# A projection stage with a five-tap convolution: its loop written out, its last tile handled in four column pieces

## What is computed

```python
h = rms_norm(x, norm_w[l])
proj = h @ w_in[l].astype(h.dtype)
...
qkv = jax.nn.silu(centred_depthwise_conv(jnp.concatenate([q, k, v], axis=-1), conv_w))
...
def centred_depthwise_conv(x, w):
    pad = (w.shape[0] - 1) // 2
    return lax.conv_general_dilated(
        x, w[:, None, :].astype(x.dtype), window_strides=(1,), padding=[(pad, pad)],
        dimension_numbers=('NWC', 'WIO', 'NWC'), feature_group_count=x.shape[-1])
```

## Time and profile before

| | us |
|---|---|
| median of three runs | 3618.07 |
| profiled execution | 3623.07 |
| its traced span | 3621.2 |
| TensorE busy in the span | 3216.5 |
| first and last matmul of `project_conv` start | 58.90, 340.10 |
| last store of `project_conv` issued | 355.23 |
| first load of `rows_prepare` issued | 360.85 |

### The profile page before, as it was taken

How to read it: one execution, slowest core, us unless ns; L and a number is a source line. 1 busy time by engine, 2 the same in 40 slices (tenths; PEclk the granted TensorE clock), 3 DMA queues, 4 the chain that set the end, 5 groups by cost and what they waited for, 6 DMA issues and landing times. The chain is left out here.

```text
span 3621.2 us, 60742 instructions
## 1 busy us (share of the span) xinstructions
PE 3216.5 (89%) x24054; PEld 2670.9 (74%) x24054; DVE 1305.8 (36%) x2502; ACT 1110.3 (31%) x2246; POOL 346.9 (10%) x344
## 2 busy tenths in 40 slices
PE   6997998886999989889599988999899969959799
PEld 5776897666999976468487777888688846648687
DVE  5454442253555536655500001221000035543333
ACT  4222332243444438711411110000111147730132
POOL 0000000232333320033000000000000011120000
PEclk8998999996999989989799999999999979979899
DMA  3221763342334333155411111110111141054443
GB/s 111 70 70 58 247 229 138 99 135 88 126 128 133 127 105 113 55 170 194 142 58 65 63 62 47 35 35 23 70 70 70 67 158 50 14 183 163 186 150 122
DMA packets 237171, 382.65 MB, mean 106 GB/s; under 512 B 37440, under 2 KB 158016, under 8 KB 227520
## 3 DMA queue, kind: packets, MB, share of 16 engines
q1 hardware_dynamic: 194848, 343.95, 27.7%
q10 hardware_dynamic: 42144, 36.18, 3.1%
HBM read 237.98 MB, written 142.08 MB: 105 GB/s over the span
## 5 line engine op out<-in xcount | busy, mean ns | idle before, releaser
L106 PE MATMUL ps_pp<-h_hi,ps_whi 128*128 128x512 f32 x512 | 200.2, 391 | 15.1 <-DVE ps_wlo L2360 15.1
L106 PE MATMUL gc_pp<-h_hi,gc_whi 128*128 128x512 f32 x512 | 200.3, 391 | 13.1 <-DVE gc_wlo L2453 13.1
L107 PE MATMUL gc_pp<-h_lo,gc_whi 128*128 128x512 f32 x512 | 200.1, 391 | 0.0
L107 PE MATMUL ps_pp<-h_lo,ps_whi 128*128 128x512 f32 x512 | 199.9, 390 | 0.0
L108 PE MATMUL ps_pp<-h_hi,ps_wlo 128*128 128x512 f32 x512 | 199.9, 390 | 0.0
L108 PE MATMUL gc_pp<-h_hi,gc_wlo 128*128 128x512 f32 x512 | 199.9, 390 | 0.0
L106 PE MATMUL pc_pp<-h_hi,pc_whi 128*128 128x512 f32 x384 | 153.5, 400 | 19.7 <-DVE pc_wlo L327 19.7
L107 PE MATMUL pc_pp<-h_lo,pc_whi 128*128 128x512 f32 x384 | 152.7, 398 | 0.0
L108 PE MATMUL pc_pp<-h_hi,pc_wlo 128*128 128x512 f32 x384 | 152.5, 397 | 0.0
L1865 POOL COPY ca_q<-ca_qr 128x512 f32 (+1 forms) x16 | 10.1, 630 | 1406.7 <-DMA ca_vr<-scratch_v_rows 1231.4
L1999 DVE CUSTOM_DVE_ANT_0 ca_neg<-ca_s,ca_bias 128x640 f32<-128x640 f32 (+4 forms) x128 | 92.0, 738 | 104.7 <-PE ca_s L1886 102.9
(11 more groups left out here) (337 smaller groups left out, 7917.1 us busy)
## 6 DMA issues: line engine op xcount, KB each, us to landing
ds_pk<-scratch_pack SPq DMA_DIRECT2D x32, 1280.0 KB, 7.7
scratch_pack<-rp_out SPq DMA_DIRECT2D x32, 512.0 KB, 2.7
scratch_sig_fm<-ps_ob SPq DMA_DIRECT2D x16, 1024.0 KB, 3.9
mb_sg<-scratch_sig_fm SPq DMA_DIRECT2D x16, 1024.0 KB, 6.9
scratch_qkv_fm<-pc_acc SPq DMA_DIRECT2D x12, 1024.0 KB, 4.8
rp_fm<-scratch_qkv_fm SPq DMA_DIRECT2D x96, 128.0 KB, 2.8
n_x<-in_x SPq DMA_DIRECT2D x16, 512.0 KB, 4.0
scratch_pack<-rp_out SPq DMA_DIRECT2D x32, 256.0 KB, 2.5
```

Source lines behind the costliest of these rows:

```text
L106: nc.tensor.matmul(out, ah, bh, start=(first and i == 0), stop=False)
L107: nc.tensor.matmul(out, ah, bl, start=False, stop=False)
```

## The change

The stage's programs are written out in Python, tile by tile, without a loop of the chip. Four things differ in what they do:

1. Weights are loaded as soon as `raw[s]` is free: up to three tiles ahead, and ahead of the store in SyncE's program.
2. ScalarE and VectorE split tile n + 2 in front of their work on tile n. ScalarE does so right after the product of tile n is done, VectorE ahead of the convolution of tile n.
3. The taps of all 12 tiles come in one load of 128 by 12 by 5 (60 floats to a partition, gathered from 12 places of 20 bytes), behind the first two weight loads. `w_in` counts the weights alone.
4. The last tile is signalled by TensorE, copied, convolved, put through SiLU and stored in four column pieces. The copies take 512 columns each; the convolved pieces are 510, 512, 512 and 514 columns wide, since a piece needs two columns of its right neighbour.

```diff
-        taps = [c.sb(f"taps{s}", [P, DN_TAPS]) for s in range(2)]
+        taps = c.sb("taps", [P, DN_TILES, DN_TAPS])
...
+        cols = [slice(g * NCOL, (g + 1) * NCOL) for g in range(GROUPS)]
+        ends = [NCOL * (g + 1) - PAD for g in range(GROUPS - 1)] + [SEQ]
+        pieces = [slice(a, b) for a, b in zip([0] + ends[:-1], ends)]
...
+            def load(n):
+                s = n % 2
+                if n >= 2:
+                    sp.wait_ge(lo_ready[s], n // 2 + START)
+                sp.dma_start(raw[s][:], w_tiles[n]).then_inc(w_in[s], 16)
+
+            load(0)
+            load(1)
+            sp.dma_start(taps[:], conv_w.rearrange("n p t -> p n t")).then_inc(taps_in, 16)
+            load(2)
+            for n in range(LAST):
+                s = n % 2
+                if n + 3 <= LAST:
+                    load(n + 3)
+                sp.wait_ge(silu_done[s], n // 2 + 1 + START)
+                sp.dma_start(out[n], acc[s][:]).then_inc(stored[s], 16)
+            for g, at in enumerate(pieces):
+                sp.wait_ge(piece_silu[g], 1 + START)
+                sp.dma_start(out[LAST][:, at], acc[LAST % 2][:, at]).then_inc(stored[LAST % 2], 16)
...
+            for n in range(LAST):
+                s = n % 2
+                act.wait_ge(product[s], n // 2 + 1 + START)
+                if n + 2 <= LAST:
+                    split_hi(n + 2)
+                nc.scalar.copy(pre[s][:, PAD:PAD + SEQ], pp[s][:]).then_inc(copied[s], 1)
+                act.wait_ge(tap_done[s], (n // 2 + 1) * DN_TAPS + START)
+                nc.scalar.activation(acc[s][:], acc[s][:], ACT.Silu).then_inc(silu_done[s], 1)
+            s = LAST % 2
+            for g in range(GROUPS + 1):
+                if g < GROUPS:
+                    act.wait_ge(piece_product[g], 1 + START)
+                    nc.scalar.copy(pre[s][:, PAD + g * NCOL:PAD + (g + 1) * NCOL],
+                                   pp[s][:, cols[g]]).then_inc(piece_copied[g], 1)
+                if g > 0:
+                    act.wait_ge(piece_tap[g - 1], DN_TAPS + START)
+                    at = pieces[g - 1]
+                    nc.scalar.activation(acc[s][:, at], acc[s][:, at], ACT.Silu).then_inc(piece_silu[g - 1], 1)
...
+            for n in range(LAST):
+                s = n % 2
+                if n + 2 <= LAST:
+                    split_lo(n + 2)
+                dve.wait_ge(copied[s], n // 2 + 1 + START)
+                dve.wait_ge(stored[s], 16 * (n // 2) + START)
+                convolve(n, slice(0, SEQ), tap_done[s], (n // 2) * DN_TAPS)
+            s = LAST % 2
+            dve.wait_ge(stored[s], 16 * (LAST // 2) + START)
+            for g, at in enumerate(pieces):
+                dve.wait_ge(piece_copied[g], 1 + START)
+                convolve(LAST, at, piece_tap[g], 0)
...
+            for g, at in enumerate(cols):
+                split_products(nc, pp[s][:, at], [(whi[s][:, k, :], wlo[s][:, k, :], hi[:, k, at], lo[:, k, at])
+                                                  for k in range(KT)]).then_inc(piece_product[g], 1)
```

More of the change, by code:

```diff
@@ L277, in project_conv @@
         stored = c.sems("stored", 2)
+        piece_product = c.sems("piece_product", GROUPS)
+        piece_copied = c.sems("piece_copied", GROUPS)
+        piece_tap = c.sems("piece_tap", GROUPS)
+        piece_silu = c.sems("piece_silu", GROUPS)
         block = c.stack.enter_context(nc.Block())
-        N = DN_TILES // 2
+        cols = [slice(g * NCOL, (g + 1) * NCOL) for g in range(GROUPS)]
+        ends = [NCOL * (g + 1) - PAD for g in range(GROUPS - 1)] + [SEQ]
+        pieces = [slice(a, b) for a, b in zip([0] + ends[:-1], ends)]
@@ L302, in _, with split_hi @@
+            sp.wait_ge(stored[0], 16 * (DN_TILES // 2) + START)
+            sp.wait_ge(stored[1], 16 * (DN_TILES // 2 - 1 + GROUPS) + START)
         @block.scalar
         def _(act):
-            def split_hi(j, s):
-                act.wait_ge(w_in[s], 32 * j + 32 + START)
+            def split_hi(n):
+                s = n % 2
+                act.wait_ge(w_in[s], 16 * (n // 2) + 16 + START)
                 nc.scalar.copy(whi[s][:], raw[s][:]).then_inc(hi_ready[s], 1)
[L308 to L321, removed]
+            for n in range(2):
+                split_hi(n)
+            for n in range(LAST):
[6 more added lines that the diff above has]
+                nc.scalar.activation(acc[s][:], acc[s][:], ACT.Silu).then_inc(silu_done[s], 1)
@@ L323, in _, with split_lo @@
         @block.vector
         def _(dve):
-            def split_lo(j, s):
-                dve.wait_ge(hi_ready[s], j + 1 + START)
+            def split_lo(n):
+                s = n % 2
+                dve.wait_ge(hi_ready[s], n // 2 + 1 + START)
                 nc.vector.tensor_tensor(wlo[s][:], raw[s][:], whi[s][:].bitcast(F32),
                                         ALU.subtract).then_inc(lo_ready[s], 1)
[L330 to L340, removed]
-                    if more:
-                        split_lo(j + 1, s)
@@ new lines, in convolve @@
+            def convolve(n, at, sem, base):
+                s = n % 2
+                nc.vector.tensor_scalar(acc[s][:, at], pre[s][:, at], taps[:, n, 0:1], None, ALU.mult).then_inc(sem, 1)
+                for t in range(1, DN_TAPS):
+                    dve.wait_ge(sem, base + t + START)
+                    nc.vector.scalar_tensor_tensor(out=acc[s][:, at], in0=pre[s][:, at.start + t:at.stop + t],
+                                                   scalar=taps[:, n, t:t + 1], in1=acc[s][:, at], op0=ALU.mult,
+                                                   op1=ALU.add).then_inc(sem, 1)
```

24 lines of the change are left out of this document (14 added, 10 removed).

## The result

The changed kernel takes 3606.11 us, the median of 20 runs (3595.32 to 3620.73), against 3622.99 us for the kernel before, also of 20 runs (3612.68 to 3640.07). The ratio is 0.9949, with a 95% interval from 0.9937 to 0.9961. It is faster, by 17 us instead of the 26 forecast, and its time lies 2 us above the range. The profiled execution of the changed kernel took 3617.24 us, 11 us more than the median, with a span of 3615.5 us; so single stages are read from it, and the whole from many executions. Three executions of kernels cut behind the scan (further down) are marked slow on record, being over 1.5% above the fastest of their set, and are kept in the means; without them the changed kernel up to the scan has a mean of 1386.0 us instead of 1387.9, and its shifted version 1390.2 instead of 1392.8.

What follows compares the result with a forecast made beforehand. TensorE, busy for 89% of the span, was taken as the bound, losing time to stalls, low clock and the stage's end. Gains of 18.2, 7.8 and 0.3 us took the 3618.07 us median to 3591.8, range 3584 to 3604.

Steps and rivals of the forecast that it cites:

- Part 1: Stalls between the changed stage's tiles: early loads and splits remove them, gain 18.2 us: 10.2 idle time, 8.0 clock.
- the rival in which its clock stays low: Parts 1 and 2 come, but TensorE still falls to 1.2 GHz now and then in the stage: 3600; chance 0.08.
- the sum: Whole kernel: 18.2 + 7.8 + 0.3 = 26.3 us gained, later stages starting earlier and otherwise the same.
- Part 2: Changed stage's end: the last tile in four pieces ends the stage earlier, gain 7.8 us.
- Part 3: Taps in one load: the first CAST no longer waits for them, gain 0.3 us; the new load costs nothing.
- Part 4: Written-out code in the changed stage: TensorE steps through 1152 matmuls without a loop, code loading put at nothing.
- The rival with slow code: TensorE's code arrives too slowly without a loop; at 50 ns more a matmul the kernel takes 3650; chance 0.04.

Runs made afterwards that it cites:

- shifted version: Changed kernel cut behind the scan, with 133 semaphore increments on TensorE spread over four gaps to move its code: mean 1392.8 us.
- tail only: Kernel before with items 3 and 4 alone, written out, weights asked for and split where the kernel before does: 3614.24 us, ratio 0.9967.
- the cut kernels: Kernel before and changed kernel with everything behind `delta_gates` left out and x copied to the output: 902.41 and 874.82 us.
- the pause: Changed kernel with six loads, one after the other, ahead of the scan: 3626.33 us, ratio 1.0004 to the kernel before.
- three pieces: Changed kernel with two piece copies ahead of tile 10's SiLU and the last tile's first two pieces made one: 3606.36 us, ratio 0.9937.

## Why the prediction was wrong

**Part 1 was right in its mechanism.** The product took 262.8 us, from 60.36 to 322.8 plus its last matmul's end, where 263.4 had been put down; against the 281.6 of the earlier trace rows that is 18.8, forecast 18.2. In this pair both halves came, the idle time and the clock, and no later stretch of the changed stage is below 1.00, so the rival in which its clock stays low fell. The casts stand at the product's end as described. (The prediction's 104.3 for the end of tile 1's product is 104.46 by the earlier trace rows; nothing rests on it.) Over all profiles the gain is a little smaller: the last matmul of the kernel before starts anywhere from 334.9 to 341.0 us (mean of seven 339.2), that of the changed kernel, in eleven profiles, within 322.1 to 323.3 (mean 322.6). That is 16.6 us. The profile on which the sum rested was 0.9 us later than the mean, and the 8.0 us put down to the clock are no fixed amount: with 21 dips at 35 stalls, what the clock takes is drawn anew in each execution.

**Part 2 was right.** Its terms against the timelines: a multiply-add 752 ns for 745, a piece 3.55 us for 3.6, the first copy at 316.02, just behind the SiLU of tile 10, the end of the last multiply-add 8.2 us behind the start of the last matmul for 8.0, the next load 13.1 for 12.9. Against 20.75 that is 7.65 us, forecast 7.8. The Trainium skill (VectorE: DVE Perf Modes, section on the TRN2 errata) would have had 691 ns for the 512 columns; the line through two measured widths was the better guide, by 54 ns. The page's formula is for an addition of two tensors, and there the trace agrees: the subtraction of `split_lo`, 1024 columns, took 1225 ns, where it gives 1224.

**Part 3** cost nothing, as said; the load of 20-byte pieces landed in 4.8 us, estimated at 5. What the taps' loads cost the kernel before was under-estimated, as tail only showed (at most 2.1 us for 0.3), but that lies inside the gain of part 1.

**Part 4.** Written out, the matmuls follow each other by 0.22 to 0.23 us, and there is no idle time marked as issue in the stage. The rival with slow code is gone.

**The step that failed** is the sentence in the sum: "The stages behind start earlier and are the same." They do start earlier: up to `delta_gates` the cut kernels are 25.5 us apart, and the sum had 26.3. They are not the same: 8.0 us of the gain, give or take 5, don't reach the end. The sum put that term at nothing, on no row; the range alone allowed some us for the clock of other stages.

Where the 8 us go isn't shown. The largest single place in the two full profiles is the scan, 14.5 us longer in the changed kernel, with 277 matmuls fewer in its first 93 us at the lower clock. But its length scatters in both kernels. In the kernel before, its cuts and shifts it took 494.3, 493.8, 501.2, 495.9, 490.4 and 506.7 us; in the changed kernel, its cuts and shifts 508.8, 513.5, 492.6, 512.9, 494.0, 508.0, 494.2 and 491.5, with the pause 503.0, with three pieces 502.4. The means, 497.1 and 502.1, are 5 us apart, give or take 8. And the times of the kernels cut ahead of the scan and behind it (25.5 and 24.3 us of gain) show no loss in it. A later start brought back nothing that can be seen, and the place of the code gave results both ways. The cause stays open.

**A second error, of size,** is the base. I took 5.0 us off the profiled time of 3623.07 because the median of three runs was 3618.07. The median of 20 is 3622.99. Without that step the forecast would have been 3596.8, and its range, 5 us higher, would have held 3606. Of the 14.3 us by which 3591.8 was too low, 4.9 are this base. The other 9.4 are the stages behind, and a part of up to 2 us by which the stage itself gives less than 26.3: 24.3 us, if the means of all profiles are taken for the product. That a range 5 us higher would have held the result says nothing for the step: the gain in it was still 26 us against 17.

## What to carry to other kernels

A stall of 2 us at each second tile of a matmul stage costs its idle time and, at some stalls, the clock as well (here at 21 of 35), and a load and split issued one tile ahead takes both away; a stage's tail behind TensorE shrinks by cutting the last tile into pieces as wide as its fixed costs allow. A gain that the stage's profile shows in full may arrive only in part at the end: here 17.5 of 25.5 us, so such a sum needs a term, and a range, for what later stages take back, even where nothing in them was changed. Single profiles of a stage whose length scatters by 20 us can't say where: that takes many executions of cut kernels. A base for a forecast of half a per cent should not be a median of three.

## What the runs showed of the hardware

- Equal code, started at the same time, got different clocks: in the same stretch of the scan, from 837 to 868 us, TensorE was granted 0.50 in one execution of the changed kernel and 0.76 in another, with 30.5 us busy in both, and did 469 and 640 matmuls. The scan took 508.8 and 492.6 us.
- An idle time of TensorE of 2.06 to 2.08 us was followed by a dip of its granted clock in some executions and not in others: in the stretch from 104 to 126 us the kernel before had 19.94 us busy, 0.92 granted and 82 matmuls in one profile, 19.92 us busy, 1.00 granted and 88 matmuls in another.
- A semaphore increment on TensorE that nothing waits for took some 0.16 us: from the first load of `rows_prepare` to TensorE's first matmul there, 123 of them took 19.2 us, 133 took 21.4 and 64 took 10.6, against 8.7 and 8.5 us without any. So it is no free filler for moving code.
- A multiply-add on VectorE of 512 columns took 752 ns, where two wider ones (2352 ns at 2048, 1281 at 1024) put 745 on their line.
